# A feed-forward, mixer and two-layer program on one core: attention probabilities of the mixer turned by DMA transposes in place of TensorE, and pack, join and eviction of the latent attention put in another order

## What is computed

```python
def hybrid_mixer(...):                      # once
    z = u @ w_in                            # gate, x, q, k, v, two merge gates
    xc = causal_depthwise_conv(x_br, conv_w, conv_b)
    y_lru = rg_lru(xc, ...) * gelu(gate_br) # gates, sqrt, associative scan
    scores = q . k / 8, masked to a window of 128, sink column
    probs = softmax(scores)[..., :-1]       # 16 heads, 4 key heads
    y_attn = probs . v
    merged = sigmoid(g_lru) * (y_lru @ w_proj_lru) + sigmoid(g_attn) * (y_attn @ w_proj_attn)
    return merged @ w_out

def hybrid_layer(...):                      # twice
    conv branch; latent attention "mla": q, k normed, gained, turned by angle, 8 heads of 96
    dilated attention "dil": 3 groups of 8 heads of 64; each softmax, then values
    return x + merged @ w_o
```

## Time and profile before

| | us |
|---|---|
| runs before, median of three | 1272.32 (1270.34 to 1272.97) |
| the profiled execution, its own time | 1272.15 |
| span in its trace | 1270.1 |
| PE busy | 1258.4 |
| DVE busy | 926.3 |
| ACT busy | 786.1 |
| POOL busy | 101.4 |

### The profile page before, as it was taken

The page is one execution under the profiler, slowest core; times in us unless marked ns, Lnnn a source line. Parts: engine busy times, 40 slices in busy tenths (PEclk is TensorE's granted clock), DMA queues, the critical chain, the costliest instruction groups (busy, mean ns, idle before and its releaser), DMA issues.

```text
span 1270.1 us, 17658 instructions
## 1 busy us (share of the span) xinstructions
PE 1258.4 (99%) x6964; PEld 1065.3 (84%) x6964; DVE 926.3 (73%) x1062; ACT 786.1 (62%) x1018; POOL 101.4 (8%) x77
## 2 busy tenths in 40 slices
PE   9999999999999999999999999999999999999999
PEld 7888888987778888888888899888888878998887
DVE  6576556687987755556677789966867887798575
ACT  7576545568756565655775876554467768656441
POOL 0000000000001100000246000000012640000000
PEclk9999999999999999999999999999999999999999
DMA  9686637542476866664577898575657797957662
GB/s 349 234 288 231 220 106 252 170 118 82 149 240 207 255 226 204 205 223 132 174 225 179 234 252 234 180 229 175 211 168 251 182 232 203 253 172 219 196 199 83
DMA packets 160962, 258.51 MB, mean 204 GB/s; under 512 B 103664, under 2 KB 103792, under 8 KB 160752
## 3 DMA queue, kind: packets, MB, share of 16 engines
q1 hardware_dynamic: 158000, 248.55, 63.4%
q10 hardware_dynamic: 2880, 8.84, 2.5%
HBM read 232.19 MB, written 1.05 MB: 184 GB/s over the span
## 4 chain that ended last, share of the span: by engine, by line
PE 77%; DVE 7%; DMA 5%; issue 3%; ACT 3%; POOL 3%; SPq 0%; ACTq 0%; another core or an unknown queue 0%; POOLq 0%; DVEq 0%
PE psum L2146 20%; PE psum L2167 20%; PE psum L2147 20%; DMA swapped<-planes 4%; PE psum L2152 4%; PE psum L2199 4%; PE psum L2153 4%; POOL rstd L639 2%; DVE w_lo L1337 2%; PE psum L2214 2%; PE psum L2345 1%; POOL mean L635 1%; DMA raw<-weights 1%; PE psum L2599 1%; DVE y_lo L1337 1%
## 5 line engine op out<-in xcount | busy, mean ns | idle before, releaser
L1337 DVE TENSOR_TENSOR w_lo<-raw,w_hi 128x1024 fp32r<-128x1024 f32 x219 | 265.3, 1222 | 119.1 <-ACT w_hi L695 118.0
L695 ACT ACTIVATE w_hi<-raw 128x1024 fp32r<-128x1024 f32 x219 | 228.5, 1054 | 122.3 <-PE psum L2167 78.7
L2146 PE MATMUL psum<-w_hi,x_hi 128*128 128x512 f32 x552 | 217.0, 393 | 0.0
L2147 PE MATMUL psum<-w_hi,x_lo 128*128 128x512 f32 x552 | 214.6, 389 | 0.0
L1337 DVE TENSOR_TENSOR y_lo<-raw,y_hi 128x1024 fp32r<-128x1024 f32 x139 | 168.6, 1221 | 42.3 <-ACT y_hi L695 41.6
L695 ACT ACTIVATE y_hi<-raw 128x1024 fp32r<-128x1024 f32 x139 | 146.0, 1055 | 60.5 <-DMA raw<-weights 28.8
L2167 PE MATMUL psum<-w_lo,x_hi 128*128 128x512 f32 x552 | 170.0, 389 | 0.0
L2146 PE MATMUL psum<-y_hi,x_hi 128*128 128x512 f32 (+1 forms) x376 | 148.0, 393 | 3.5 <-ACT arena L1213 3.5
L2147 PE MATMUL psum<-y_hi,x_lo 128*128 128x512 f32 (+1 forms) x376 | 146.9, 391 | 0.0
L2146 PEld LDWEIGHTS psum<-w_hi,x_hi 128*128 128x128 f32 x552 | 103.8, 188 | 22.9 <-issue 1.6
L2167 PEld LDWEIGHTS psum<-w_lo,x_hi 128*128 128x128 f32 x552 | 103.7, 188 | 21.6 <-DVE w_lo L1337 0.3
(11 more groups left out here) (229 smaller groups left out, 2317.0 us busy)
## 6 DMA issues: line engine op xcount, KB each, us to landing
raw<-weights SPq DMA_DIRECT2D x406, 512.0 KB, 4.4
probs<-weights SPq DMA_DIRECT2D x8, 512.0 KB, 5.3
probs_t<-weights SPq DMA_DIRECT2D x8, 512.0 KB, 5.2
arena<-gains ACTq DMA_DIRECT2D x7, 512.0 KB, 4.6
arena<-gate_bias ACTq DMA_DIRECT2D x6, 512.0 KB, 4.2
norm<-x_feat SPq DMA_DIRECT2D x4, 256.0 KB, 5.2
res<-x SPq DMA_DIRECT2D x2, 512.0 KB, 8.5
arena<-lru_w ACTq DMA_DIRECT2D x1, 1024.0 KB, 4.9
```

Source lines behind the costliest of these rows:

```text
L695: act.activation(slot(t)[0], raw_place(t), ACT.Copy).then_inc(hi_ready, 1)
L1337: dve.tensor_tensor(lo, raw_place(t), hi.bitcast(F32), ALU.subtract).then_inc(lo_ready, 1)
L2146: pe.matmul(out_, l_hi, r_hi, start=start, stop=False, skip_group_check=skip)
L2147: pe.matmul(out_, l_lo, r_hi, start=False, stop=False, skip_group_check=skip)
```

## The change

In the mixer the eight PE transposes and the two copies of each unit are gone. ACT packs the scaled probabilities into `planes` (`mix_pack`), SP transposes them ahead of tiles 102, 106, 108, 112, 114 and 118, and DVE joins them into `probs_t` in the next chunk, ahead of that chunk's mask (`mix_join`). The values of a unit move from after the first tile of the next chunk to after its second. The order of the turned blocks in `probs_t` is now that of the planes, so the moving operand of the value matmuls is a strided view; their number and size stay. The mask of a unit waits until the unit before has been packed, and a join until the values before have been made.

In the layers no work is added or removed. The transfer of dil 3 is issued ahead of tile 39 in place of 40; ACT packs mla 1 behind the `dil_v` eviction of c = 8 in place of the end of c = 7, and packs dil 4 ahead of `mla_gain(1)`; DVE joins dil 3, mla 3 and dil 4 later in their chunks.

The diff, without dropped semaphores and functions that only change place:

```diff
@@ -392,11 +392,11 @@
                 + [("dil", 4), ("unit", 0), ("dil", 5)] + [("unit", u) for u in range(1, UNITS_LAYER)])
-        SWAP_AT = (22, 32, 36, 40, 42, 44, 46, 48, 50, 52, 55, 56, 59, 63, 67, 70, 74, 78, 82)
+        SWAP_AT = (22, 32, 36, 39, 42, 44, 46, 48, 50, 52, 55, 56, 59, 63, 67, 70, 74, 78, 82)
 
         def job(kind, n, l):
 
-            return At(JOBS.index((kind, n)) + 1, l, len(JOBS))
+            return At(len(UNITS1) + JOBS.index((kind, n)) + 1, l, len(JOBS))
@@ -410,8 +410,11 @@
 
-        LAYER_SWAPS = {At(LAYER_AT, l, LAYER_TILES) + at: job(*what, l)
+        PLANE_SWAPS = {At(LAYER_AT, l, LAYER_TILES) + at: job(*what, l)
                        for l in range(LAYERS) for what, at in zip(JOBS, SWAP_AT)}
+
+        MIX_SWAP_AT = (36, 40, 42, 46, 48, 52)
+        PLANE_SWAPS.update({MIX_AT + at: u + 1 for u, at in enumerate(MIX_SWAP_AT)})
@@ -599,10 +599,10 @@
                                            ).then_inc(hidden_swapped, 16)
-                if t in LAYER_SWAPS:
-                    sp.wait_ge(planes_packed, LAYER_SWAPS[t])
-                    if LAYER_SWAPS[t] > 1:
-                        sp.wait_ge(planes_joined, LAYER_SWAPS[t] - 1)
+                if t in PLANE_SWAPS:
+                    sp.wait_ge(planes_packed, PLANE_SWAPS[t])
+                    if PLANE_SWAPS[t] > 1:
+                        sp.wait_ge(planes_joined, PLANE_SWAPS[t] - 1)
                     sp.dma_start_transpose(swapped.rearrange("p (b s) -> p b s", s=P), planes[:, :]
@@ -899,12 +899,6 @@
 
-            def probs_copy(u):
-                if u == 4:
-                    return
-                act.wait_ge(probs_turned, u)
-                act.activation(probs_t[:, 0:512], psum[:, 4, :], ACT.Copy).then_inc(probs_act, 1)
-
             def chunk_done(at):
@@ -944,6 +938,24 @@
 
+            def planes_free(count):
+
+                if count > 1:
+                    act.wait_ge(planes_swapped, 16 * (count - 1))
+
+            def planes_pack(count, words):
+
+                planes_free(count)
+                act.activation(by_plane(planes), by_word(words.bitcast(U16)), ACT.Copy).then_inc(planes_packed, 1)
+
+            def mix_pack(u):
+
+                if u < UNITS1_BY_DVE:
+                    act.wait_ge(probs_normed, u + 1)
+                else:
+                    act.wait_ge(probs_scaled, u - UNITS1_BY_DVE + 1)
+                planes_pack(u + 1, probs[:, :])
+
             def heads_copy(e):
@@ -1059,10 +1069,17 @@
                     scale_probs(u)
+                    mix_pack(u)
                 refill(t + 3)
+                if c == 6:
+                    mix_pack(u)
                 if c in (7, 8):
                     act.wait_ge(conv_done, 2)
+                    if c == 8:
+                        mix_pack(u)
                     decay_tanh(c - 7)
+                    if c == 7:
+                        mix_pack(u)
                     decay(c - 7)
@@ -1211,6 +1218,7 @@
                         act.activation(dil_v[:, 0, :, :], pair(fill_of(c - 1)), ACT.Copy).then_inc(act_freed, 1)
+                        mla_pack(1)
                     if c in (9, 10):
@@ -1244,8 +1252,8 @@
                     if c == 9:
+                        dil_pack(4)
                         mla_gain(1)
-                        dil_pack(4)
                     if c == 10:
@@ -1266,8 +1274,6 @@
                     refill(t + 3)
-                    if c == 7:
-                        mla_pack(1)
                     if c == 8:
@@ -1526,12 +1532,12 @@
 
-            def probs_copy(u, blocks):
-                dve.wait_ge(probs_turned, u)
-                if u == 4:
-                    dve.tensor_copy(probs_t[:, 0:512], psum[:, 4, :]).then_inc(probs_act, 1)
-                n = (blocks - 4) * P
-                dve.tensor_copy(probs_t[:, 512:512 + n], psum[:, 5, 0:n]).then_inc(probs_dve, 1)
+            def mix_join(u):
+
+                dve.wait_ge(planes_swapped, 16 * (u + 1))
+                if u:
+                    dve.wait_ge(values_ready, u)
+                dve.tensor_copy(by_word(probs_t.bitcast(U16)), by_plane(swapped)).then_inc(planes_joined, 1)
@@ -1735,9 +1739,13 @@
                     heads_rest(2)
+                if 1 <= u <= len(UNITS1):
+                    mix_join(u - 1)
                 if 0 <= u < len(UNITS1):
                     qt, heads = UNITS1[u]
                     n = len(heads)
+                    if u:
+                        dve.wait_ge(planes_packed, u)
                     mask_scores(At(u + 1), qt, n, mask_window)
@@ -1942,8 +1948,6 @@
                         dil_join(c - 4)
-                    if c == 9:
-                        mla_join(3)
                     if c == 11 or c == 12:
@@ -2005,11 +2009,11 @@
                             negated_max(len(heads), width).then_inc(max_ready, 1)
+                    if c == 9:
+                        mla_join(3)
                     refill(t + 1)
                     if c == 7:
                         mla_join(0)
-                    if c == 9:
-                        dil_join(4)
                     if 1 <= u <= UNITS_LAYER:
@@ -2044,9 +2048,10 @@
                         dve.sem_inc(mla_ready, 1)
-                        dil_join(3)
                     if c == 8:
                         mla_join(2)
+                    if c == 9:
+                        dil_join(4)
                     if c == 10:
@@ -2081,6 +2086,8 @@
                         step.sync()
+                    if c == 6:
+                        dil_join(3)
                     if c == 7:
@@ -2345,17 +2352,6 @@
 
-            def probs_read(u):
-                pe.wait_ge(probs_act, u)
-                pe.wait_ge(probs_dve, u)
-
-            def turn_probs(ready, u, places):
-                pe.wait_ge(ready, u)
-                for b, at in enumerate(places):
-                    ins = turn(wide(4, 1024)[:, at * P:(at + 1) * P], probs[:, b * P:(b + 1) * P])
-                ins.then_inc(probs_turned, 1)
-
-
             def warm(n):
@@ -2376,25 +2372,19 @@
 
-            def places1(qt):
-
-                if qt == 0:
-                    return range(8)
-                return [4 * i + 2 * s + j for i in range(2) for j in range(2) for s in range(TOK)]
-
             def values1(u):
 
                 qt, heads = UNITS1[u]
-                probs_read(At(u + 1))
+                pe.wait_ge(planes_joined, u + 1)
                 if u in (2, 4):
                     pe.wait_ge(heads_lo, u // 2)
                 n = len(heads) // 2 * P
                 bank, at = ((6, 0), (7, 0), (6, 0), (6, n), (7, 0), (7, n))[u]
+                turned = probs_t.rearrange("p (i j s n) -> p i s j n", i=2, s=qt + 1, n=P)
                 for s in range(qt + 1):
                     for i in range(2):
-                        first = (i * (qt + 1) + s) * n
-                        ins = pe.matmul(psum[i * HEAD:(i + 1) * HEAD, bank, at:at + n], v_cols(min(heads) + i, s),
-                                        probs_t[:, first:first + n], start=s == 0, stop=s == qt)
+                        out_ = psum[i * HEAD:(i + 1) * HEAD, bank, at:at + n].rearrange("p (j n) -> p j n", n=P)
+                        ins = pe.matmul(out_, v_cols(min(heads) + i, s), turned[:, i, s], start=s == 0, stop=s == qt)
                 ins.then_inc(values_ready, 1)
@@ -2459,7 +2449,7 @@
                     if u:
-                        probs_read(At(u))
+                        pe.wait_ge(max_ready, At(u))
                     else:
@@ -2505,12 +2495,8 @@
                         unit_scores()
-                    if q == 0 and 1 <= u <= len(UNITS1):
+                    if q == 1 and 1 <= u <= len(UNITS1):
                         values1(u - 1)
-                if 0 <= u < len(UNITS1):
-                    by_dve = u < UNITS1_BY_DVE
-                    turn_probs(probs_normed if by_dve else probs_scaled, u + 1 if by_dve else u - UNITS1_BY_DVE + 1,
-                               places1(UNITS1[u][0]))
                 if c == 6:
```

More of the change, by code:

```diff
@@ L503, in block_program @@
         probs_scaled = sem("probs_scaled")
-        probs_turned = sem("probs_turned")
-        probs_act = sem("probs_act")
-        probs_dve = sem("probs_dve")
         planes_packed = sem("planes_packed")
@@ L995, in _ @@
                                    scale=HEAD ** -0.5).then_inc(q_copied, 1)
-                if 0 <= u - 1 < len(UNITS1):
-                    probs_copy(At(u))
                 if c == 7:
@@ L1132, in dil_square @@
                     act.activation(probs[:, :], norm[:, (j + 1) % 2, :], ACT.Square).then_inc(dil_squares, 1)
-                def planes_free(count):
-                    if count > 1:
-                        act.wait_ge(planes_swapped, 16 * (count - 1))
                 def mla_pack(n):
@@ L1154, in mla_gain @@
                     act.activation(k_, k_, ACT.Copy, scale=lp[0:QK, L_GCOL + 1:L_GCOL + 2]).then_inc(mla_copied, 1)
-                def planes_pack(count, words):
```

(6 more changed lines are left out.)

## The result

| | before | changed |
|---|---|---|
| median of the runs, us | 1272.56 (1270.34 to 1272.97, 4 runs) | 1284.37 (1283.49 to 1285.66, 4 runs) |
| profiled execution, us | 1272.15 | 1285.66 |
| span in the trace, us | 1270.1 | 1283.9 |

The ratio is 1.0105, 95% interval 1.0088 to 1.0121: slower by 11.8 us in the medians. The forecast was 1278.3, with a range to 1284.0; the sign was right, the size half of what came. A second set of runs of the changed kernel gave 1282.96 (1281.64 to 1283.84, 4 runs) against 1270.24, ratio 1.010 (1.0087 to 1.0114).

The account below looks back on a forecast made before the run. PE looked like the bound, but only because PE, DVE and ACT are level late in the mixer. Mixer +7.6, layers -3.0 and clock +1.7 make +6.3 on 1272.15, given as 1278.3 us; own range 1274.2 to 1281.9, overall 1270.5 to 1284.0.

Parts of the forecast that it names:

- The mixer: Mixer: packs and joins lengthen the chain through ACT and DVE to c = 12; +7.6 us, bounds +5.0 and +9.3.
- Joins: Mixer, DVE: joins of units 2, 3 and 4 lengthen the chain by 1.35, 1.35 and 0.66 us.
- Packs: Mixer, ACT: packs of units 1 and 2 add 2.6 us together, that of unit 3 adds 1.9.
- The transposes: Mixer, PE: removing 48 transposes, 6.3 us busy, gains nothing because PE waits for the recurrence at c = 11 and 12.
- The DMA cover: Mixer: transfers standing in SP's queue of loads cost nothing, as the DMA share there is 0.24 to 0.58.
- The layers: Both layers: eviction waits go and first latent scores shift, +0.45 - 1.1 - 2.3 = -3.0 us, before the clock.
- Clock: Layers: a PE pause of about 3 us ahead of each layer's latent scores, half clock at even chances; +1.7 us.
- First scores of layer 1: First layer: latent scores come at 704.95 instead of 706.03, -1.1 us.
- A: Layers: latent chain not late, eviction waits and clock loss go, -8.3 us; with the mixer's +7.6, 1271.5; chance 0.10.
- B: Mixer: half of its growth is absorbed, 3.8 us left; sum +2.5, 1274.6; chance 0.08.
- C: Mixer: PE is the bound, packs and joins fall into gaps, PE sheds 6.3 us; sum -7.6, 1264.6; chance 0.15.
- D: Mixer: transfers fall behind loads, land after 7.7 us, DVE stands in c = 10 to 12; +6.3 + 5.1, 1283.6; chance 0.12.

Follow-up runs that it names:

- mixer_only: The changed kernel with the layers' order, packs and joins as before, so only the mixer's part is changed: 1280.59 us, ratio 1.008 against the kernel before.
- layers_only: The kernel before with only the layers' part of the change, the mixer as before: 1271.99 us, ratio 1.0013 against the kernel before.
- one_turn: The kernel before with seven of each unit's eight PE transposes left out (42 of 48, probabilities wrong): 1272.58 us, ratio 1.0020.
- pack1_only_new_mixer: The changed kernel with one edit, ACT packing mla 1 at the end of c = 7 again: 1275.2 us, ratio 1.0035 against the kernel before.
- root_first: The changed kernel with the mixer's pack of c = 9 behind the square root instead of ahead: 1283.2 us, ratio 1.0096 against the kernel before.

## Why the prediction was right and wrong

**The mixer: right in size, and mostly in its terms.** +7.6 forecast, +7.3 measured in every trace of that mixer (7.22 to 7.31). The root's product moved by 6.3 - 1.4 = 5.0 ("some 5 us"), the low half of c = 11 by 6.2 and that of c = 12 by 6.8. Joins: 3.4 forecast (1.35 + 1.35 + 0.66), 3.4 given back when cut. Packs: 1.3 + 1.3 + 1.9 and the last values' share, with 4.8 in the expectation of the cut; 4.1 measured. The transposes: 0 forecast, 1.0 measured, which stands against the packs and joins. "I give them nothing" was 1 us too low. The DMA cover held: no join in the changed mixer stood for its landing; PE stood 5.2 us for the join of c = 10. One figure is open: the median of `mixer_only` lies 2.4 us above what the stage says.

**The layers: the waits at the evictions right, the sum wrong.** -3.0 for the waits and +1.7 for the clock were forecast, -1.3. The two traces of the changed kernel lie 5.8 and 3.1 us above the mean of the two of before in the layers, 4.5 on average; by the medians it is 1.0 to 3.1. The sign was wrong by either. Set against the profile of before, on which I summed, the first trace has +4.8: first scores +1.2 and +0.5, from there to the start of c = 10 another 3.2 and 3.1 (the clock), then -1.2 and -2.0 for the waits at 1219. Of the 6.1 us between +4.8 and -1.3, 4.6 are the clock and 2.3 the first scores of layer 1, less 0.9 that the waits gave more. So two terms failed.
- *Clock*: "Two pauses at even chances: +1.7, bounds 0 and +3.4." A stretch followed each of the four layer pauses of the changed kernel, three of them with 6.83 us, worth up to 3.4 and not 1.7. The upper bound should have been twice as high, and the chances nearer to one than to even. I had read even chances from a single wait of 1.32 us; pauses near 3 us had no counter-example in the trace. My price for the short stretch does not follow from the row as written (five more products of 0.225 us are 1.1), but 1.7, half of 3.41, is what came: in `layers_only` PE lost 1.7 and 1.6 us between the first scores and c = 10, in the changed kernel's second trace 1.7 (a short stretch) and 2.4 (a long one).
- *First scores of layer 1*: "the same working gives scores at 704.95". In the changed kernel they came at 716.14 - 8.91 = 707.2, 2.3 us late. The second layer's came at 1054.15 - 12.17 = 1042.0, as the text had it (1041.95; its own terms add up to 1041.86). The eviction and the pack stand right behind the split that waited 3.43 us for weights (shown above), and so their time is set by that landing. I had taken it as free: on ACT's order I counted instructions ahead of the pack, not the landings they wait for. The size varies: in the changed kernel's second trace the scores came at 705.7 and in `layers_only` at 705.9. In the first trace the pack of mla 0 was already late, at 689.1 against 687.5 and 687.3 in these two; why is not shown.

The waits at 1219 went, as forecast; forecast at 2.3 us, they gave 1.2 and 2.0 by the tiles behind them.

**The base.** I summed against the profiled 1272.15 and set the median 0.2 above it. The later medians of before were 1269.8 to 1271.3. The trace shown had a half-clock stretch in the first layer, which three of the four others with the old order of the layers lack, and an early start (others up to 1.5 us later). A single profile carries about 2 us of such luck in this kernel, near 0.2% of the time.

**The rivals.** A, B and C are refuted for the change as it stands: the layers gained nothing, the mixer's growth was not halved, and PE was not the mixer's bound. But A's reason, that earlier transfers pull the chain ahead, is what the last runs show: with mla 1's pack left where it was the same layers gain 8.8 us (A had 8.3), and what stood against A, three steps behind the later pack, is what undid it. D gave nearly the right time, 1283.6, for the wrong reason: no join in the changed mixer stood for a landing. The real loss lay in none of them.

The weighing with the Trainium skill ("VectorE: DVE Perf Modes", Rules for kernel authors: TensorE for such a transpose where PSUM will do) turned out as the row did: the old way was cheaper here, by the mixer's 7.3 us. The Trainium skill's page "TensorE: Matmul & The Clock Gate" (Why this matters for your kernels) warns of TensorE idle gaps between bursts of matmuls. This case's traces agree (a half-clock stretch came with every pause of 2.8 us or more), and the warning would have put the clock term higher than I did.

## What to carry to other kernels

When an instruction is moved to stand behind others, list what each of those waits for, weights' splits included; an engine that no longer stands for one landing may stand for the next, with a longer chain behind it. Price a pause of TensorE of some 3 us (one of 2 us in part) as its length plus the half clock that comes with it, unless TensorE waits again right behind, and fill it with a piece of independent work. When a change bundles several moves, run each alone: one move here hid 8.8 us that the others gain. Work taken off a full TensorE is worth only what the other engines' chain leaves, and what is put on that chain in exchange counts in full.

## What the runs showed of the hardware

Over all traces, 25 pauses of TensorE of 2.8 us or more (in mixer and layers) were each followed by, or ended in, a stretch at a granted 0.50. Of nine between 1.8 and 2.6 us four were, and none of the 1.7 us ones ahead of 2435. A single long pause is not needed: `one_turn` had a stretch in its mixer behind two waits of only 0.9 and 0.8 us, close together.

The stretch lasted 3.41 us in 11 of the 25 cases and 6.83 in 14, for one kernel at the same place too: 6.83 in the changed kernel's first layer, 3.41 in its second trace. It was the long one in all 14 cases where it began before the pause had ended, and the short one in the 11 where it began after.

This makes runs of one kernel differ. `pack1_only_new_mixer` had one of 1280.85 among nine of 1273.56 to 1276.43. That run has no trace, but its mean granted clock was 0.993, against 0.996 to 0.997 in the nine, an estimated 8 to 10 us more at half clock (0.003 to 0.004 of the span, doubled). In `root_first` the three runs with 0.992 took 1283.20 to 1284.64, the two with 0.994 and 0.996 1279.79 and 1280.27.
